# Turning the value tiles to tokens: two bursts per in-projection, or one tile behind each of five panels

## The reference, cut to what matters

```python
for l in range(DEPTH):                                   # DEPTH = 2
    zx = modulate(rms_norm(x, norm1_g[l]), mx[0], mx[1])
    zc = modulate(rms_norm(h, norm1_g[l]), mc[0], mc[1])
    rq, rk, rv, rg, aq, ak, av, cu, cv = split_in(zx @ w_in[l])
    crq, crk, crv, crg, caq, cak, cav, ccu, ccv = split_in(zc @ w_in[l])
    # retention reads rv and crv, windowed attention av and cav, chunk gating cv (and ccv in layer 0)
    ...
    x = x + mx[2] * (concat(ret_x, att_x, cm_x) @ w_out[l])
    x = x + mx[5] * swiglu(modulate(rms_norm(x, norm2_g[l]), mx[3], mx[4]), w_gate[l], w_up[l], w_down[l])
    # the context stream h gets the same treatment in layer 0 only
return rms_norm(x, final_norm_g)
```

## Time and profile before

| what | value |
|---|---|
| median of three runs | 1851.55 us (1849.31 to 1853.04) |
| the profiled execution, its own time | 1851.66 us |
| its span, first to last instruction | 1849.9 us |
| what lies around the span | 1.8 us |
| granted clock of PE, mean over the span | 0.940 |
| busy share: PE, DVE, POOL, ACT | 89%, 45%, 33%, 32% |
| DMA | 155.24 MB, mean 84 GB/s |

### The profile page before, as it was taken

One profiled execution on the slowest core, in us unless ns is written; L12 is line 12 of the kernel. 1 busy time (PEld: TensorE's weight loads), 2 busy tenths in 40 slices (PEclk: granted clock), 3 DMA queues, 4 the chain that ended last, 5 costly groups with the idle time before them and its releaser, 6 DMA issues.

```text
span 1849.9 us, 25723 instructions
## 1 busy us (share of the span) xinstructions
PE 1643.8 (89%) x10030; PEld 1360.8 (74%) x10030; DVE 827.6 (45%) x1335; ACT 593.2 (32%) x1013; POOL 615.1 (33%) x331
## 2 busy tenths in 40 slices
PE   4799985778989999999999998996679799999997
PEld 2587764446777888888888887775447688888986
DVE  3632153662432232332223254516463667677675
ACT  4212223652253111111111116322652543333433
POOL 0722231001214232322223221333103377676771
PEclk8799997889989999999999998998799899999999
DMA  6554440000214322123332210221000323233221
GB/s 234 178 182 137 136 114 1 1 1 24 90 69 160 114 92 91 61 97 113 113 113 91 68 46 23 69 68 46 1 1 24 114 86 96 91 111 93 76 83 46
DMA packets 122195, 155.24 MB, mean 84 GB/s; under 512 B 20352, under 2 KB 89872, under 8 KB 122128
## 3 DMA queue, kind: packets, MB, share of 16 engines
q1 hardware_dynamic: 122128, 154.32, 26.0%
HBM read 152.21 MB, written 2.10 MB: 83 GB/s over the span
## 4 chain that ended last, share of the span: by engine, by line
PE 73%; DVE 13%; ACT 5%; issue 5%; SPq 2%; DMA 1%; POOL 1%; DVEq 0%; ACTq 0%; POOLq 0%
PE ps L1831 12%; PE ps L1832 12%; PE ps L1833 11%; PE ps L2143 3%; PE ps L2144 3%; PE ps L2145 3%; PE ps L2240 2%; PE ps L2242 2%; PE ps L2241 2%; PE ps L1756 2%; PE ps L2029 2%; PE ps L2255 2%; PE ps L2051 2%; PE ps L2257 2%; PE ps L2256 2%
## 5 line engine op out<-in xcount | busy, mean ns | idle before, releaser
L516 POOL TENSOR_TENSOR wl<-raw,wh 128x1024 fp32r<-128x1024 f32 (+1 forms) x182 | 364.3, 2011 | 761.1 <-ACT wh L638 760.9
L1831 PE MATMUL ps<-zh,wh 128*128 128x512 f32 x1248 | 437.8, 351 | 10.4 <-POOL zl L516 5.7
L1832 PE MATMUL ps<-zl,wh 128*128 128x512 f32 x1248 | 434.7, 348 | 0.0
L1833 PE MATMUL ps<-zh,wl 128*128 128x512 f32 x1248 | 430.6, 345 | 0.0
L1831 PEld LDWEIGHTS ps<-zh,wh 128*128 128x128 f32 x1248 | 237.8, 191 | 73.5 <-issue 32.3
L638 ACT ACTIVATE wh<-raw 128x1024 fp32r<-128x1024 f32 (+1 forms) x182 | 155.3, 869 | 342.8 <-PE ps L1833 251.0
L1833 PEld LDWEIGHTS ps<-zh,wl 128*128 128x128 f32 x1248 | 237.0, 190 | 31.6
L1832 PEld LDWEIGHTS ps<-zl,wh 128*128 128x128 f32 x1248 | 237.7, 190 | 28.6
L1689 DVE TENSOR_TENSOR hf<-gs,ps 128x512 f32<-128x512 f32 (+1 forms) x44 | 22.4, 551 | 269.9 <-ACT gs L1051 269.9
L516 POOL TENSOR_TENSOR wl_d<-raw_d,wh_d 128x1024 fp32r<-128x1024 f32 x42 | 100.2, 2408 | 117.7 <-ACT wh_d L638 117.7
L1708 DVE SCALAR_TENSOR_TENSOR xT<-ps,modcol,xT 128x512 f32<-128x512 f32 (+1 forms) x176 | 104.1, 616 | 63.2 <-PE ps L2145 61.8
(11 more groups left out here) (286 smaller groups left out, 3003.9 us busy)
## 6 DMA issues: line engine op xcount, KB each, us to landing
raw<-in_w_gate_dram SPq DMA_DIRECT2D x22, 1024.0 KB, 5.5
raw<-in_w_up_dram SPq DMA_DIRECT2D x22, 1024.0 KB, 6.6
raw_m<-in_w_mod_dram SPq DMA_DIRECT2D x22, 1024.0 KB, 5.0
raw_d<-in_w_down_dram SPq DMA_DIRECT2D x21, 1024.0 KB, 4.9
raw<-in_w_in_dram SPq DMA_DIRECT2D x14, 1024.0 KB, 5.4
raw<-in_w_mod_dram SPq DMA_DIRECT2D x11, 1024.0 KB, 5.3
raw_n<-in_w_mod_dram SPq DMA_DIRECT2D x9, 1024.0 KB, 5.2
raw<-in_w_out_dram SPq DMA_DIRECT2D x32, 256.0 KB, 4.4
```

The costliest lines, as they stand in the source:

```text
L516: nc.gpsimd.tensor_tensor(dst, src, hi.bitcast(F32), ALU.subtract).then_inc(sem(done), 1)
L1831: MM(dst, wt_h[:, h, w], zh[:, k, c0:c1], start=(k == 0), stop=False)
L1832: MM(dst, wt_h[:, h, w], zl[:, k, c0:c1], start=False, stop=False)
L1833: last = MM(dst, wt_l[:, h, w], zh[:, k, c0:c1], start=False, stop=(k == KC - 1))
```

## The change

Tile v of the values is now turned behind a panel of its own: tile 0 behind panel 1, tile 1 behind panel 2, tile 2 behind panel 3, tile 3 behind panel 5 and tile 4 behind panel 6 (`TOKENS_AT`). All use banks 5 (latent) and 6 (context); bank 7 is no longer written by a tile, and the wait for `modcol_rdy` is gone, as is the wait for `vtr_ev` behind panel 3. Each tile still waits for the copy of the tile before, and PE still waits for the fifth copy ahead of panel 7. ACT copies a tile out right behind the evacuation of that panel's second half. Panels 4 to 6 are written out one by one in PE's stream instead of a loop. The counts of transposes, copies, matmuls and DMAs are the same.

```diff
--- before.py
+++ after.py
@@ -43,7 +43,10 @@
 NP_IN = len(PANELS)
 NP_CTX = 3
 
-V_AT, CV_AT = 3, 6
+CV_AT = 6
+
+
+TOKENS_AT = {1: 0, 2: 1, 3: 2, 5: 3, 6: 4}
 
 
 R_N1, R_N2, R_NF, R_RN, R_CN, N_ROWS = 0, 16, 32, 40, 44, 48
@@ -838,19 +841,15 @@
 
                 def to_tokens_out(p):
 
-                    if p == V_AT:
-                        for v in range(3):
-                            act.wait_ge(sem(f"vtr_mm{l}"), v + 1)
-                            cols = slice(P * v, P * v + P)
-                            copy(vtok[:, 4:6, cols], ps[:, 7, 0:SC].rearrange("p (t n) -> p t n", t=2))
-                            copy(vtok[:, 0:4, cols], ps[:, 5 + v % 2, :].rearrange("p (t n) -> p t n", t=4)).then_inc(sem(f"vtr_ev{l}"), 1)
-                    if p == CV_AT:
-                        for v in range(2):
-                            act.wait_ge(sem(f"vtr_mm{l}"), 4 + v)
-                            cols = slice(P * v, P * v + P)
-                            if l == 0:
-                                copy(cvt[:, 4:6, cols], ps[:, 7, 0:SC].rearrange("p (t n) -> p t n", t=2))
-                            copy(cvt[:, 0:4, cols], ps[:, 5 + v % 2, :].rearrange("p (t n) -> p t n", t=4)).then_inc(sem(f"vtr_ev{l}"), 1)
+                    if p not in TOKENS_AT:
+                        return
+                    v = TOKENS_AT[p]
+                    act.wait_ge(sem(f"vtr_mm{l}"), v + 1)
+                    dst, w = (vtok, v) if v < 3 else (cvt, v - 3)
+                    cols = slice(P * w, P * w + P)
+                    if v < 3 or l == 0:
+                        copy(dst[:, 4:6, cols], ps[:, 6, 0:SC].rearrange("p (t n) -> p t n", t=2))
+                    copy(dst[:, 0:4, cols], ps[:, 5, :].rearrange("p (t n) -> p t n", t=4)).then_inc(sem(f"vtr_ev{l}"), 1)
 
                 for p, name in enumerate(PANELS):
                     for h in range(2):
@@ -1870,31 +1869,29 @@
                 if l == 0:
                     mod_half(0, raw[1], 1, 2)
                     mod_half(1, raw_n, 5, 1)
-                in_step(1, True, slot=1)
-                for p in range(2, NP_CTX):
-                    in_step(p, True)
-                in_step(NP_CTX, l == 0)
-
-                def to_tokens(v, slot, ctx, order):
-                    pe.wait_ge(sem(f"ev_in{l}"), order)
+                def to_tokens(p):
+
+                    v = TOKENS_AT[p]
+                    slot, ctx = (v, True) if v < 3 else (v - 3, l == 0)
+                    pe.wait_ge(sem(f"ev_in{l}"), (1, 2, 6, 9, 10)[v])
                     if v:
                         pe.wait_ge(sem(f"vtr_ev{l}"), v)
-                    if l == 0:
-
-                        pe.wait_ge(sem("modcol_rdy"), J_IN + (V_AT if v < 3 else CV_AT))
                     for t in range(6 if ctx else 4):
-                        dst = ps[:, 5 + (v % 3) % 2, P * t:P * t + P] if t < 4 else ps[:, 7, P * (t - 4):P * (t - 4) + P]
+                        dst = ps[:, 5, P * t:P * t + P] if t < 4 else ps[:, 6, P * (t - 4):P * (t - 4) + P]
                         last = TR(dst, vT[:, slot, P * t:P * t + P], eye)
                     last.then_inc(sem(f"vtr_mm{l}"), 1)
 
-                for v in range(3):
-                    to_tokens(v, v, True, 6)
-
-                pe.wait_ge(sem(f"vtr_ev{l}"), 3)
-                with pe.Fori(V_AT + 1, CV_AT + 1) as p:
-                    in_step(p, l == 0)
-                for v in range(2):
-                    to_tokens(3 + v, v, l == 0, 10)
+                in_step(1, True, slot=1)
+                to_tokens(1)
+                in_step(2, True)
+                to_tokens(2)
+                in_step(3, l == 0)
+                to_tokens(3)
+                in_step(4, l == 0)
+                in_step(5, l == 0)
+                to_tokens(5)
+                in_step(6, l == 0)
+                to_tokens(6)
 
                 pe.wait_ge(sem(f"vtr_ev{l}"), 5)
                 with pe.Fori(CV_AT + 1, NP_IN) as p:
```

## The result

The changed kernel takes 1833.99 us (median of four runs, 1832.41 to 1836.13) against 1851.62 us before: 17.6 us less, a ratio of 0.9907 with a 95% interval of 0.989 to 0.9924. The profiled execution took 1832.44 us with a span of 1830.5 us, 19.4 us under the span before.

What follows compares the result with a forecast made beforehand. PE was taken to bound the kernel, held up in relays of turning and copying tiles. 11.5 us of waiting and 3.9 of clock, together 15.4 us off 1851.66, gave 1836 us, range 1832 to about 1843.

Steps and rivals of the forecast that it cites:

- the likeliest case: Whole kernel: the forecast with either clock outcome behind panel 6 of layer 1, 1834 to 1838 us, chance 0.65.
- Layer 0, panel 3 to 4: One group of transposes left instead of three: 5.11 us less, 1.46 back behind panels 1 and 2, net 3.65.
- Layer 0, panel 6 to 7: One copy wait instead of two: 1.84 us less, net 1.11 after tile 3's move, plus 1.40 of clock.
- Layer 1, panel 3 to 4: One group left, no idle time: net 5.80 us of waiting after 1.46 back, plus 2.51 of clock.
- Layer 1, panel 6 to 7: One idle time of 2.06 us left: 1.39 us less, net 0.95; none of 1.74 us of clock counted.
- A group's price: PE's time for a tile that waits for nobody: 0.73 us for six transposes, 0.44 for four.
- Nothing lost elsewhere: DMA, POOL and ACT: no new waits, loads start earlier with the panels, copies fit in ACT's idle time; no cost.
- The chain at the end: End of layer 1's in-projection: PE's 4.9 us wait for ACT moves as a block, so the gain reaches the end.
- The rival that all of the clock comes back: All clock falls vanish: 17.2 us gained, 1834.5 us; inside the 0.65 given to either outcome at the last gap.
- none comes back: Both layers: the clock is regained nowhere, 11.5 us of waiting remain, 1840.2 us; chance 0.15.
- the hidden layer: Work behind hides layer 1's part: only 6.2 us gained, 1845.5 us; chance 0.13 together with loads becoming the bound.
- the slower one: Clock falls behind each of the ten places where a tile is turned, 2.51 us each: 1859.6 us; chance 0.03.

Runs made afterwards that it cites:

- The filler: Kernel before, with matmuls that nobody reads put into the idle times of layer 1's two relays (turn a tile, copy it, turn the next): 1846.09 us.
- layer 0 alone: Kernel before with the tiles spread in layer 0 only; layer 1 keeps its tiles together behind panels 3 and 6, without the wait ahead of panel 4: 1844.29 us.
- tiles 3 and 4 alone: Kernel before with only tiles 3 and 4 spread, behind panels 5 and 6; tiles 0 to 2 together behind panel 3, no wait ahead of panel 4: 1843.03 us.
- layer 1 alone: Kernel before with the tiles spread in layer 1 only; layer 0 keeps its tiles together behind panels 3 and 6, without the wait ahead of panel 4: 1837.23 us.
- the fourfold tiles: Changed kernel with each tile turned four times over, to the same place: 1850.98 us.

## Why the prediction was right

Forecast 1836, range 1832 to 1843, measured 1834.0: the likeliest case, at its better end. Point by point, each from the first transpose at the place to the end of the half behind it:

- *Layer 0, panel 3 to 4:* 5.11 forecast; 14.33 us became 159.40 - 150.28 = 9.12, so 5.21.
- *Layer 0, panel 6 to 7:* 1.84 and 1.40 of clock forecast, 3.24; 13.86 became 10.63, so 3.23. The clock came back behind one idle time of 1.25 us, as argued from its like in the earlier trace rows.
- *Layer 1, panel 3 to 4:* 7.26 and 2.51 forecast, 9.77; 15.94 became 1192.87 - 1186.74 = 6.13, so 9.81. The filler shows that the split was off: some 1.2 us that I had put down to waiting were transposes at 1.2 GHz (1.44 and 1.51 instead of 0.85). And 0.3 us of the wait ahead of panel 4, here and in layer 0, were the entry into the loop, which I had put at nothing.
- *Layer 1, panel 6 to 7:* 1.39 forecast and nothing of the 1.74 of clock; 11.23 became 8.22, so 3.01. **This is the mis-sized term.** I reasoned that 2.06 us of idle time would drop the clock since 1.91 had done so the earlier trace rows. It did not, in three profiles of three. The step from one idle time to a fall was wrong. In the earlier trace rows the clock did fall behind the relay's first idle time, at 1195.0; but the same 1.91 us, and 1.05 behind them, passed at 1.00 at the same place in the runs with layer 0 alone and with tiles 3 and 4 alone. The length of an idle time doesn't decide it, and what does stays open.
- *A group's price:* 0.73 forecast, 0.63 measured, 0.36 for four (0.44 forecast): the starts are 0.105 us apart, not 0.12. Single transposes took up to 0.33 us, where I had said none would be over 0.3. Over seven groups of six that is 0.7 us, the second mis-sized term.
- *Nothing lost elsewhere:* ACT is never found waiting for a transpose, PE never for `wl`, the same loads as before come later than ACT (that for panel 6 at 180.71) and still in time for PE, and the wait behind layer 1 is 4.9 us as before. The chain at the end moved as a block: 17.76 us at the last latent copy of layer 1 (1267.18 to 1249.42).

15.4 + 1.7 + 0.7 = 17.8 us, against 17.7 in the two in-projections and 17.6 between the medians. The waiting was found where the forecast had it, place by place. That the clock's part fits so closely is in part luck: the forecast took it from one profile, and the same layer 0 took 2.7 us more in the two profiles in which the clock fell behind panel 3 as well. The rival that all of the clock comes back (1834.5) was the one that came true. The others are out: that none comes back by the low clock of 0 in three profiles, the hidden layer by the run with layer 1 alone, the slower one by the fourfold tiles.

## What to carry to other kernels

Where PE turns a tile, waits for its copy and turns the next, spread the tiles over places with a whole panel of matmuls between them: the price falls to the issue of the transposes, 0.6 us for six of 128 x 128, and the same banks will do for all. Here PE never waited for a copy ahead of a tile. Look at the granted clock in the half behind such a relay as well as at the relay: here about 5 of layer 1's 11 us were the clock. Take a second and a third profile before counting on such a fall, since the same relay may pass without one. And judge a change of a few us by its own stretch of the profile too, since the stretches behind can give it back.

## What the runs showed of the hardware that was not expected

- The clock stayed at 2.4 GHz through 2.84 us of transposes with 1.26 us of idle time behind them, and through a single idle time of 2.06 us. Yet it fell to 1.2 GHz in relays of idle times between 0.96 and 1.91 us: in layer 1 in both profiles of the kernel with unaltered relays, in layer 0 behind panel 3 in two of three.
- The same groups and the same idle times (0.82 us of transposes, then 1.91 us idle) dropped the clock in those two profiles and did not in two others, in which panel 3 ended 6 to 10 us earlier in the span. What differed ahead of them was not found.
- Entering a loop straight behind a wait cost PE 0.30 us; its rounds cost nothing.
- With 1.2 to 1.9 us taken out ahead of it, the stretch between the layers was some 2 us longer, in both profiles (885.4 and 886.0 against 883.5 to 884.1 for the changed kernel). The cause is open.
